# A two-block model on one core: the layers of the second block meet by halves of the tokens, and two feed-forward tiles are formed token by token

## The reference

```python
def rms_norm(x, g):
    x32 = x.astype(jnp.float32)
    y = x32 * lax.rsqrt(jnp.mean(x32 * x32, axis=-1, keepdims=True) + EPS)
    return (y * g.astype(jnp.float32)).astype(x.dtype)

def swiglu(u, w1, w3, w2):
    return (jax.nn.silu(u @ w1) * (u @ w3)) @ w2

    for l in range(DEPTH_2):
        h = h + 0.5 * swiglu(rms_norm(h, ffn1_norm[l]), ffn1_w1[l], ffn1_w3[l], ffn1_w2[l])
        h = h + token_mixer_2(rms_norm(h, mix_norm[l]), w_in[l], ...)
        h = h + 0.5 * swiglu(rms_norm(h, ffn2_norm[l]), ffn2_w1[l], ffn2_w3[l], ffn2_w2[l])
    return rms_norm(h, final_norm)
```

## Time and profile before

| what | us |
|---|---|
| median of 3 runs (2465.24 to 2467.74) | 2466.28 |
| the profiled execution | 2461.69 |
| its span in the trace | 2459.9 |
| busy TensorE in the span | 2046.9 (83%) |
| busy VectorE | 822.5 (33%) |
| busy ScalarE | 597.8 (24%) |

### The profile page before, as it was taken

How to read it: one execution, slowest core, us unless ns; L and a number is a source line. 1 busy time by engine, 2 the same in 40 slices (tenths; PEclk the granted TensorE clock), 3 DMA queues, 4 the chain that set the end, 5 groups by cost and what they waited for, 6 DMA issues and landing times.

```text
span 2459.9 us, 30094 instructions
## 1 busy us (share of the span) xinstructions
PE 2046.9 (83%) x12642; PEld 1426.6 (58%) x12642; DVE 822.5 (33%) x1079; ACT 597.8 (24%) x715; POOL 0.2 (0%) x4
## 2 busy tenths in 40 slices
PE   7999898766666666666666799999999999989998
PEld 2477574312122121222221799887999899888998
DVE  3412533000000000000000655566554655556554
ACT  2311201000000000000000533463333433464333
POOL 0000000000000000000000000000000000000000
PEclk9999998888877878888888999999999999999999
DMA  8325445899999999999999445433445445433552
GB/s 337 120 107 217 193 162 236 370 429 428 429 428 429 428 429 429 428 429 428 429 428 429 151 177 200 166 127 145 175 176 193 181 181 185 158 138 137 178 199 95
DMA packets 46900, 658.22 MB, mean 268 GB/s; under 512 B 5200, under 2 KB 5584, under 8 KB 6736
## 3 DMA queue, kind: packets, MB, share of 16 engines
q1 hardware_dynamic: 44640, 646.99, 65.0%
q10 hardware_dynamic: 2160, 9.78, 1.0%
HBM read 655.71 MB, written 1.05 MB: 267 GB/s over the span
## 4 chain that ended last, share of the span: by engine, by line
PE 58%; DMA 32%; DVE 5%; ACT 3%; issue 2%; ACTq 0%; SPq 0%; DVEq 0%
PE ps L1142 57%; DMA ring<-stream_dram 17%; DMA ring_b<-stream_dram 15%; PE ps L1151 1%; ACT w_hi L540 1%; DVE att_area L1061 0%; DVE mixer_area L1065 0%; DVE ring_lo L995 0%; ACT expert_area L520 0%; ACT area_n L377 0%; DMA tail<-filt_dram 0%; ACT att_area L608 0%; DVE tail L829 0%; DVE area_n L662 0%; DVE tail L836 0%
## 5 line engine op out<-in xcount | busy, mean ns | idle before, releaser
L995 DVE TENSOR_TENSOR ring_lo<-ring,w_hi 128x2048 fp32r<-128x2048 f32 x174 | 398.6, 2292 | 241.9 <-ACT w_hi L540 241.2
L1142 PE MATMUL ps<-u_hi,w_hi 128*128 128x256 f32 x1664 | 473.5, 285 | 4.5 <-DVE u_lo L1002 4.5
L1142 PE MATMUL ps<-u_hi,ring_lo 128*128 128x256 f32 x1664 | 471.1, 283 | 0.0
L1142 PE MATMUL ps<-u_lo,w_hi 128*128 128x256 f32 x1664 | 471.1, 283 | 0.0
L540 ACT CAST w_hi<-ring 128x2048 fp32r<-128x2048 f32 x174 | 331.7, 1908 | 217.8 <-PE ps L1142 217.6
L1142 PEld LDWEIGHTS ps<-u_hi,w_hi 128*128 128x128 f32 x1664 | 319.3, 192 | 8.2 <-DVE u_lo L1002 5.8
L1142 PEld LDWEIGHTS ps<-u_lo,w_hi 128*128 128x128 f32 x1664 | 319.4, 192 | 1.6
L1142 PEld LDWEIGHTS ps<-u_hi,ring_lo 128*128 128x128 f32 x1664 | 319.4, 192 | 0.0
L1142 PE MATMUL ps<-ring,area_h 128*32 128x512 f32 (+1 forms) x1088 | 177.5, 722 | 78.4 <-DMA ring<-stream_dram 69.9
L1142 PE MATMUL ps<-ring_b,area_h 128*32 128x512 f32 x1024 | 153.0, 741 | 92.1 <-DMA ring_b<-stream_dram 83.6
L965 DVE TENSOR_TENSOR expert_area<-expert_area,ps 128x512 f32<-128x512 f32 x16 | 11.0, 687 | 454.2 <-PE ps L1142 454.2
(11 more groups left out here) (281 smaller groups left out, 2026.7 us busy)
## 6 DMA issues: line engine op xcount, KB each, us to landing
ring<-stream_dram SPq DMA_DIRECT2D x212, 2048.0 KB, 13.1
ring_b<-stream_dram SPq DMA_DIRECT2D x96, 2048.0 KB, 34.9
tail<-filt_dram ACTq DMA_DIRECT2D x1, 1728.0 KB, 7.2
tables<-tabs_dram ACTq DMA_DIRECT2D x1, 1408.0 KB, 10.1
tabs<-tabs_dram ACTq DMA_DIRECT2D x1, 1296.0 KB, 6.0
x_tok<-x_dram ACTq DMA_DIRECT2D x1, 1024.0 KB, 16.3
area_n<-ctx_dram ACTq DMA_DIRECT2D x1, 1024.0 KB, 23.2
fin_rows<-fin_rows_dram ACTq DMA_DIRECT2D x2, 512.0 KB, 4.4
```

The costliest lines, as they stand in the source:

```text
L995: V.tensor_tensor(ring_lo[:, n % RING, :], ring[:, n % RING, :], w_hi[:, n % SPLITS, :].bitcast(F32), ALU.subtract).then_inc(sig("w_ready" ...
L1142: ins = M.matmul(out, lhsT, rhs, start=start, stop=stop, **more)
```

## The change

- The layer loop is written out (`for l in range(LAYERS)`), so waits are on constants and there is no branch between the layers.
- The gains of the norms are no longer a scale on features after the turn. They come as a row on all partitions (`norm_row`, 512 KB, loaded by six transfers from ScalarE's queue, one a stage ahead for each norm), and the norm's second instruction multiplies by it. The turned input is then copied plainly: for each half two instructions of 512 columns on each of ScalarE and VectorE.
- The last two slots of a stage (down 9 and down 10; the last two of the mixer's four output slots) are taken by halves (`two_halves`): both slots for t = 0, then both for t = 1. The eight transposes of the next stage's t = 0 stand ahead of the last three matmuls of t = 1 (`turn_half`).
- The first two slots of a stage are one loop over halves (`first_two`): the t = 0 half is multiplied while the norm of t = 1 is made, and its transposes stand after six of eight feature blocks. In the feed-forward stages the first two up slots change their layout: tokens are stationary and 512 columns (256 of `w1`, 256 of `w3`) move, so the hidden values come with tokens on partitions, and four transposes after up 2 turn them, with a copy on ScalarE and two subtractions on VectorE.
- Since both first slots are in use at once, a fourth buffer for upper parts is taken (`ALONE`: slots 1, 34 and 55, in `att_r`). The other slots go through the three buffers in turn (`IN_TURN`). Slots 0 to 2 of layer 0 are cast before the first block's last norm.

One cast of a weight slot now stands between the first half's square and the copies of its turned blocks. The diff, cut to its core:

```diff
-DOWN_STEPS = FT // 2 + 1
+DOWN_STEPS = FT // 2
+ALONE = (1, MIX_AT + 1, FFN_AT[1] + 1)
+IN_TURN = [n for n in range(SPLIT_SLOTS) if n not in ALONE]
+PLACE = {n: i for i, n in enumerate(IN_TURN)}
...
+        def upper_part(n):
+            return att_r[:, 0:SLOT] if n in ALONE else w_hi[:, PLACE[n] % SPLITS, :]
...
+            def upper(l, n):
+                turn = l * (LAYER_SLOTS // RING) + (LAYER_TURNS + n // RING)
+                act.wait_ge(sig(f"pair_loaded{n % RING // 2}"), turn * 16 + 16)
+                base = l * LAYER_SLOTS + LAYERS_AT
+                if n == ALONE[2]:
+                    act.wait_ge(sig("slot_used"), base + MIX_AT + 17)
+                elif n == ALONE[1]:
+                    act.wait_ge(sig("slot_used"), base + ALONE[0] + 1)
+                elif l == 0 and n in (0, 1, 2, 3):
+                    act.wait_ge(sig("slot_used"), LAYERS_AT - RING)
+                elif n == ALONE[0]:
+                    act.wait_ge(sig("slot_used"), base - LAYER_SLOTS + ALONE[2] + 1)
+                elif PLACE[n] >= SPLITS:
+                    act.wait_ge(sig("slot_used"), base + IN_TURN[PLACE[n] - SPLITS] + 1)
+                else:
+                    act.wait_ge(sig("slot_used"), base - LAYER_SLOTS + IN_TURN[PLACE[n] - SPLITS] + 1)
+                A.copy(upper_part(n), ring[:, n % RING, :]).then_inc(
+                    sig("alone_hi_ready") if n in ALONE else sig("w_hi_ready"), 1)
...
+            for n in range(3):
+                upper(0, n)
...
-            with act.Fori(0, LAYERS) as l:
-                step = Link(act, sig("act_layer_step"), l, 6)
...
+            for l in range(LAYERS):
+                def square(n, t):
+                    at = l * 3 + n
+                    if t == 0:
+                        A.activation(stat[:, 2, 0:1], col("eps"), ACT.Sqrt)
+                    act.wait_ge(sig("h_ready"), at * TT + t + 1)
+                    step(A.activation(xn[:, t, :], x_tok[:, t, :], ACT.Square, accum_out=stat[:, 0, t:t + 1]))
+                    A.activation(stat[:, 0, 2 + t:3 + t], stat[:, 0, t:t + 1], ACT.Sqrt, scale=1.0 / D,
+                                 bias=col("eps")).then_inc(sig("rms2_ready"), 1)
+                def upper_turned(n, t):
+                    for b in range(2):
+                        act.wait_ge(sig("uT_ps"), (l * 3 + n) * 4 + t * 2 + b + 1)
+                        A.copy(u_hi[:, 4 * b:4 * b + 4, t * P:(t + 1) * P],
+                               bank(2 * t + b).rearrange("p (k q) -> p k q", k=4)).then_inc(sig("u_hi_ready"), 1)
+                def begin(n, before):
+                    if before is None:
+                        square(n, 0)
+                        square(n, 1)
+                        upper_turned(n, 0)
+                        upper_turned(n, 1)
+                    else:
+                        square(n, 0)
+                        upper_next(*before[0])
+                        upper_turned(n, 0)
+                        square(n, 1)
+                        upper_turned(n, 1)
+                    if n == 0:
+                        act.dma_start(lcols[:, :], d["lcols"][l]).then_inc(sig("lcols_loaded"), 16)
+                    if n == 0 or n == 2 and l + 1 < LAYERS:
+                        act.dma_start(norm_row, d["norm_rows"][l * 3 + n + 1]).then_inc(sig("norm_row_loaded"), 16)
+                    if before is None:
+                        upper(0, 3)
+                    else:
+                        upper_next(*before[1])
...
+                            if i == 2:
+                                act.wait_ge(sig("hidT_ps"), l * 2 + f + 1)
+                                A.copy(hid_hi[:, 0:2, :],
+                                       bank(0).rearrange("p (i t) -> p i t", i=2)).then_inc(sig("hidT_hi"), 1)
...
+                        if n == 28 and f == 0:
+                            upper(l, ALONE[1])
+                        elif n == 28 and l + 1 < LAYERS:
+                            upper(l + 1, ALONE[0])
...
+                def norm(n, t):
+                    at = l * 3 + n
+                    dve.wait_ge(sig("rms2_ready"), at * TT + t + 1)
+                    step(V.reciprocal(stat[:, 0, t:t + 1], stat[:, 0, 2 + t:3 + t]))
+                    dve.wait_ge(sig("norm_row_loaded"), at * 16 + 16)
+                    V.scalar_tensor_tensor(xn[:, t, :], x_tok[:, t, :], stat[:, 0, t:t + 1], norm_row,
+                                           ALU.mult, ALU.mult).then_inc(sig("norm2_ready"), 1)
+                def lower_turned(n, t, b):
+                    dve.wait_ge(sig("u_hi_ready"), (l * 3 + n) * 4 + t * 2 + b + 1)
+                    u = slice(4 * b, 4 * b + 4), slice(t * P, (t + 1) * P)
+                    V.tensor_tensor(u_lo[:, u[0], u[1]], bank(2 * t + b).rearrange("p (k q) -> p k q", k=4),
+                                    u_hi[:, u[0], u[1]].bitcast(F32), ALU.subtract).then_inc(sig("u_ready"), 1)
+                def add_ffn(done, t):
+                    dve.wait_ge(sig("down_step"), done * DOWN_STEPS - 1 + t)
+                    V.scalar_tensor_tensor(x_tok[:, t, :], two_banks(2 * t), 0.5, x_tok[:, t, :],
+                                           ALU.mult, ALU.add).then_inc(sig("h_ready"), 1)
+                def add_mixer(done, t):
+                    dve.wait_ge(sig("mixer_ps"), (done - 1) * TT + t + 1)
+                    V.tensor_tensor(x_tok[:, t, :], two_banks(2 * t), x_tok[:, t, :],
+                                    ALU.add).then_inc(sig("h_ready"), 1)
+                def begin(n, add, done):
+                    if add is None:
+                        norm(n, 0)
+                        norm(n, 1)
+                        lower_turned(n, 0, 0)
+                        lower_turned(n, 0, 1)
+                    else:
+                        add(done, 0)
+                        norm(n, 0)
+                        lower_turned(n, 0, 0)
+                        add(done, 1)
+                        lower_turned(n, 0, 1)
+                        norm(n, 1)
+                    lower_turned(n, 1, 0)
+                    lower_turned(n, 1, 1)
...
+                def turn_half(at, t):
+                    pe.wait_ge(sig("norm2_ready"), at * TT + t + 1)
+                    for k in range(KD):
+                        turn(bank(2 * t + k // 4)[:, k % 4 * P:(k % 4 + 1) * P], xn[:, t, k * P:(k + 1) * P],
+                             ready=sig("uT_ps") if k % 4 == 3 else None)
...
+                def first_two(at, n, ready):
+                    w = [split(n)]
+                    for t in range(TT):
+                        for k in range(KD):
+                            if t == 0 and k == 4:
+                                w.append(split(n + 1))
+                            if t == 0 and k == 6:
+                                turn_half(at, 1)
+                            a = (k % 4) * 512
+                            product3(bank(4 + t), turned(at, t, k), [v[:, a:a + 512] for v in w[k // 4]],
+                                     k == 0, k == KD - 1, free=int(t == 1 and k % 4 == 3),
+                                     ready=ready if k == KD - 1 else None)
+                def two_halves(w, x, k0, k1, ready, after):
+                    for t in range(TT):
+                        for i in range(2):
+                            v = w[i](t)
+                            for j in range(2):
+                                k = k0 + 2 * i + j
+                                for c in range(2):
+                                    a = j * 1024 + c * 512
+                                    last = j == c == 1
+                                    if t == i == 1 and last and after is not None:
+                                        turn_half(after, 0)
+                                    product3(bank(2 * t + c), [h[:, t * P:(t + 1) * P] for h in x(k)],
+                                             [u[:, a:a + 512] for u in v], k == 0, k == k1 - 1,
+                                             free=int(last and t == 1), ready=ready if last and i == 1 else None)
...
+                            pair(w, bank(4 + i % 4), sig("ffn_ps"))
+                            if i == 2:
+                                pe.wait_ge(sig("hid_mid"), base + 2)
+                                for t in range(TT):
+                                    for j in range(2):
+                                        turn(bank(0)[:, j * T + t * P:j * T + (t + 1) * P], hid[:, t, j * P:(j + 1) * P],
+                                             ready=sig("hidT_ps") if t == j == 1 else None)
...
+                    def last_two(i):
+                        def w(t):
+                            if t == 0:
+                                pe.wait_ge(sig("hid_done"), base + FT - 2 + 2 * i)
+                            return split(at + 31 + i)
+                        return w
+                    two_halves([last_two(0), last_two(1)], x, FT - 4, FT, sig("down_step"), after)
+                ffn(0, 0, l * 3 + 1)
```

(13 more changed lines are left out.)

315 lines of the change are left out of this document (152 added, 163 removed).

## The result

| | us |
|---|---|
| before, median of 4 runs (2460.75 to 2467.74) | 2465.76 |
| the changed kernel, median of 4 runs (2430.31 to 2435.41) | 2433.09 |
| ratio, with its 95% interval | 0.9876 (0.9863 to 0.989) |
| profiled execution after, and its span | 2430.31, 2428.4 |

By the medians the change saves 32.7 us; the profiled executions differ by 31.4. The forecast was 27 and a time of 2439; the range from 2431 to 2449 holds the measured time.

The account below looks back on a forecast made before the run. TensorE is saturated inside feed-forward stages and waits at seams for the sum-to-turn chain. Terms 4.3 + 2 x 3.7 + 7.3 + 5.9 + 1.5 + 2.4 - 2.4 = 26.4, called 27: 2466.3 - 27 = 2439 us; 2431 to 2449 (8 in 10).

Parts of the forecast that it names:

- seams 1 to 5: Stage borders in the layers where TensorE waits; forecast savings 4.3, 3.7, 7.3, 5.9 and 3.7 us in turn.
- seam 3: Border between the layers: saves 7.3 us, counting VectorE's 3.25 us idle as the hardware loop's price.
- first two up slots: Feed-forward stages: 96 matmuls of 256 columns (11.51 us) become 48 of 512 (10.91), four times: 2.4 us saved.
- seam 0: Border from first block to layers: first square 1.6 us earlier, no early half; 1.5 us saved besides the new layout.
- hidden turns: Turning hidden values in feed-forward stages: four transposes and an operand change, some 0.6 us, four times: -2.4.
- the mixers: Mixer stages: waits on constants drop some register instructions from their chains, part of rounding 26.4 to 27 us.
- A seam's cost: TensorE time at each overlapped stage border: two groups of transposes plus idle of 0.6 and 0.15, 2.65 us.
- X: Moment when TensorE has issued all t = 0 work of a stage's last two slots; 24 matmuls (5.45 us) follow.
- The median shown is 4.6 above it: Last step: the old median stands 4.6 us above its profiled execution, so 27 is taken from 2466.3, giving 2439.
- The half chains come late: Rival: chains 1 us late at five seams give back 10 us; saving 17, time 2449; chance 0.17.
- More is gained: Rival: mixer chains shorten more, or seam 0's clock comes up earlier; saving 32 to 37, 2429 to 2434; chance 0.10.
- The fourth buffer's cast: Rival: this cast, waiting for its transfer, holds up ScalarE in three places; 2507 us at slow landing; chance 0.03.

Follow-up runs that it names:

- last_two_by_slot: The changed kernel, but a stage's last two slots are done one after the other, each for both token halves; median 2449.91 us, ratio to before 0.995.
- turn_both_first: The changed kernel, but TensorE turns the second token half ahead of the new stage's first product, not behind 18 matmuls; 2461.88 us, ratio to before 0.9991.
- places_kept: The changed kernel with 24 unused columns put back so all buffers behind them lie at their old addresses; 2431.63 us, ratio to before 0.9871.
- before_again: The kernel before, unchanged, timed against itself and profiled a second time; median 2464.55 us, ratio 1.0004.
- unrolled_only: The kernel before with only the layer loop written out on ScalarE, VectorE and TensorE; median 2464.03 us, ratio to before 1.0005.
- cast_first: The changed kernel with the next weight slot's cast ahead of the first half's square in ScalarE's list; 2463.21 us, ratio to before 0.9998.
- clock_kept: The changed kernel with 20 matmuls of constants into an unused bank ahead of seam 0's first turns; 2439.57 us, ratio to before 0.9899.
- best: The changed kernel with a 24-column gap ahead of the token operands and eleven matmuls of constants at seam 0; 2429.36 us, ratio to before 0.9841.

## Why the forecast was right, and where it was off

**The mechanism** is as forecast: no wait over 0.6 us at seams 1 to 5, clock 1.00, turns ahead of the last three matmuls, and VectorE's 3.25 us of idle at seam 3 gone. last_two_by_slot and turn_both_first take away the lead and its use, one at a time, and each gives back what its idle says and the slow clock behind it. The new layout of the first two up slots and the longer norm were not tried alone; they are read from the timelines.

**The sum's terms**, in us, from the two first profiles:

| term | forecast | measured |
|---|---|---|
| seam 1 | 4.3 | 6.99 - 2.11 = 4.9 |
| seams 2 and 5 | 7.4 | 2 x (6.33 - 2.11) = 8.4 |
| seam 3 | 7.3 | 9.91 - 2.11 = 7.8 |
| seam 4 | 5.9 | 4.7 + 1.8 = 6.5 |
| seam 0 | 1.5 | 2.33 less its layout = 1.8 |
| first two up slots | 2.4 | 4 x 0.54 = 2.2 |
| hidden turns | -2.4 | 4 x -0.36 = -1.4 |
| the mixers | 0, or +0.6 in "call it 27" | -0.5 and -1.9 |
| the rest of the feed-forward stages | 0 | -0.5 |
| layers' part | 26.4 | 27.3 |

That the sum is so close is in part luck: seams 1 to 5 gave 2.7 more than forecast, and the mixers took 2.4 back.

- *A seam's cost*, forecast 2 x 0.95 + 0.6 + 0.15 = 2.65, is 2.11: eight turns delay the next matmul by 0.79, not 0.95, the idle ahead of the first new matmul is 0.52, and the 0.15 ahead of the second turn does not occur. The add of the second half starts at X + 6.72 by the row above, not X + 6.95. That is 2.7 us over five seams. The cast between square and copy was placed 0.7 us behind its slot's use, though the row named there (1707.70 to 1707.91) gives 0.2; it came 0.3 behind, which only widened the slack.
- *The first two up slots* came out near the forecast (0.54 each, not 0.60) by two errors that cancel. Their 96 matmuls had been costed at the pace inside a stage, 11.51, but took 11.80, as four of their first intervals are 0.18 to 0.23 and not 0.12, and the 48 new ones took 11.26 without the turns' 0.79, not 10.91. In places_kept they took 11.09. So 0.17 of that miss are the addresses, as the change moved the operands and the forecast costed the shorter `lcols` at nothing; most of the other 0.18 are the two late matmuls behind the wait and behind the turns. At seam 2, the first matmul of up 2 before (up 0 begins at 1719.48 there), then the first of up 0 and of up 2 after:
```profile
1731.28 0.28 PE L1142 MATMUL ps<-u_hi,w_hi 128*128 128x256 f32 x1
1704.10 0.47 PE L1267 MATMUL ps<-w_hi,u_hi 128*128 128x512 f32 x1 [0.35 <-DVE u_lo L1083]
1716.15 0.28 PE L1267 MATMUL ps<-u_hi,w_hi 128*128 128x256 f32 x1
```
- *Hidden turns*: 0.36 each (from 1381.83 to 1382.19 in the first tile), not 0.6, and no wait.
- *The mixers* were to shorten by a fraction and got longer, without their seams by 0.5 and 1.9 us. In the second one the profile of before had a granted clock of 0.99 (2125 to 2259 us; 0.97 in the first mixer, and 0.97 in both after), and against before_again its loss is 0.6; so 1.2 of the 1.9 are again a profile of before that ran fast. The cause of the 0.5 is open. The shortening that was to come from waits on constants does not show in unrolled_only either, where the waits are on constants too: from its first matmul to its last the mixer took 148.04 and 148.55 us there, 148.05 and 148.48 before.
- *Seam 3 at 7.3 and not 4.* The row of 3.25 us of idle is the loop's, as unrolled_only shows. The trace agrees with the rule quoted from the Trainium skill in that the idle goes with the loop; that the fetch of instructions was behind it, no run shows. But what the loop's end was worth depended on what stood behind it: alone nothing, with the halves all of its 9.9 us wait went but 2.1.

**The step that failed for the median** is the last one: "The median shown is 4.6 above it", carried over unchanged to the new kernel. The 4.6 were not a constant: the changed kernel's medians lie 2.8 above, 4.6 below and 0.2 above its three profiled executions. Of the 4.4 us by which the first of these (2430.31) beats the forecast 2434.7, 4.2 are the first block's, which no term of the sum touches, and the measured 2433.09 lies outside the narrow forecast of 2434 to 2443. So the hit of the median is in part luck. Another part is the clock behind the old seams: the second profile of before, the slowest of its eleven runs, has 7.5 us more in its layers, of which 5.3 lie from seam 1 to seam 4, where the change closes the waits, and 2.5 behind seam 0, where it does not (the stretch behind seam 4 gives 0.3 back). The changed kernel's layers' part stays within 1077.8 to 1078.0 in three profiles. So by these five profiles the change takes away the waits and also scatter behind them, and the medians saved 32.7, 28.0 and 33.3 us in three comparisons where the layers of the two first profiles say 27.3. How much of the first comparison's 32.7 is this and how much the first block's scatter (1350.6 to 1359.4 in one kernel) four runs each can't say.

**The rivals.** *The half chains come late*: no; slack is 0.4 us at the first turn and 0.2 at the second (1557.2 against 1557.41). Its price, 1 us for each us of lateness, was set too low: cast_first, with the first half alone 4.4 us late, costs 6.0 per seam, since the clock fell in each of these waits too, and in last_two_by_slot even 2.3 us of idle was followed by a fallen clock three times in five. *More is gained*, the 0.10 rival, gives the measured time of 2433, but not by its mechanisms: the mixers did not shorten, and seam 0's first six new matmuls still ran at half clock. *The fourth buffer's cast* waited for a transfer for 2.1 us in six casts together, with nothing late on TensorE:
```profile
L553 ACT CAST att_r<-ring 128x2048 fp32r<-128x2048 f32 x6 | 11.4, 1903 | 2.1 <-DMA ring<-stream_dram 2.1
```

## What to carry to other kernels

A stage border on a saturated TensorE cost the whole chain sum, norm, turn, split here, until a part of the tokens was finished some 5 us before the rest and there was work of the new stage to do on it. Both were needed, and one misplaced 1.9 us instruction in ScalarE's list, at five seams, undid all of it. Count a removed wait twice, once as itself and once as the clock that may fall behind it, and compare a profile with a second one before its distance to the median is taken as fixed. When a change resizes a buffer, look whether the pace of the matmuls moved with the addresses.

## What the runs showed of the hardware that was not expected

- Matmul pace depends on where in SBUF the operands lie: 0.228 to 0.233 us for 512 columns and 0.118 to 0.120 for 256, in four placements that differ by 32 to 96 bytes. The rule behind it is open.
- At seam 0 TensorE's last matmul ended at 1350.5; the granted clock was 1.00 up to 1354, 0.88 on average from 1354 to 1356 and 0.50 from 1356. In last_two_by_slot it fell to 0.50 behind idle of only 2.3 us, at three seams of five. With matmuls of constants in the wait it stayed at 1.00 (clock_kept and best).
- Eight transposes between matmuls of 512 columns delayed the next matmul by 0.79 us, four between matmuls of 256 columns by 0.36.
- The end of a hardware loop of two turns kept VectorE idle for 3.25 us (3.22 in before_again); with the loop written out this was gone.
